# A norm row and a pool-scale row spread by TensorE, gate weights loaded later, two tanh buffers in the tail

## The reference

```python
u = rmsnorm(x, norm_mix);  proj = u @ w_in          # 1024 x 5632
xl, gl, xp, gp, ml, mp = split(proj)
xc = causal_conv(xl)                                # width 4, per channel
r, i = sigmoid(xc @ w_rg_a + b_a), sigmoid(xc @ w_rg_i + b_i)   # 16 blocks of 64x64
log_a = -8 * r * softplus(-lam);  a = exp(log_a)
b = sqrt(1 - a*a) * i * xc;  h = scan(a, b)         # h_t = a_t h_(t-1) + b_t
lru_out = h * silu(gl)
pooled = trailing means of xp over 2/4/8/16 frames, minus xp
pool_out = (pooled @ w_pool + b_pool) * pool_scale * silu(gp)
merged = sigmoid(ml) * lru_out + sigmoid(mp) * pool_out
x = x + merged @ w_out
x = x + sigmoid(rmsnorm(x, norm_ple) @ w_ple_gate) * (p @ w_ple)
y = rmsnorm(x, final_norm)
```

## Time and profile before

| | |
|---|---|
| median of 3 runs shown | 1083.83 us (1073.97 to 1114.7) |
| the profiled execution, its own time | 1074.5 us |
| its span on the slowest core (core 7) | 1072.9 us; the eight cores 1061.6 to 1072.9 |
| busy share of the span | PE 90%, DVE 81%, ACT 74%, POOL 49% |
| mean granted TensorE clock | 0.964 to 0.971 on the eight cores |
| moved by DMA | 188.5 MB per core, 176 GB/s over the span |

### The profile page before, as it was taken

One profiled execution on the slowest core, in us unless ns is written; L12 is line 12 of the kernel. 1 busy time (PEld: TensorE's weight loads), 2 busy tenths in 40 slices (PEclk: granted clock), 3 DMA queues, 4 the chain that ended last, 5 costly groups with the idle time before them and its releaser, 6 DMA issues.

```text
span 1072.9 us, 17836 instructions; the slowest of 8 cores (1061.6 to 1072.9 us)
## 1 busy us (share of the span) xinstructions
PE 963.2 (90%) x4655; PEld 442.4 (41%) x4655; DVE 869.9 (81%) x1224; ACT 796.2 (74%) x1299; POOL 521.4 (49%) x621
## 2 busy tenths in 40 slices
PE   1588988985799999999999999999999999999892
PEld 1233433432344445444444444454444454444340
DVE  3447878897468898899989998899988898979752
ACT  4468888875368888887888778888788877688442
POOL 2113334433336664566554555555666546545554
PEclk9888999988899999999999999999999999999996
DMA  7897798556767784668566475657466655453441
GB/s 220 200 206 227 208 236 231 158 158 199 170 184 210 190 235 124 174 179 215 162 180 175 134 224 158 184 160 198 145 188 166 173 166 160 123 181 119 128 101 78
DMA packets 186663, 188.54 MB, mean 176 GB/s; under 512 B 81273, under 2 KB 131705, under 8 KB 186565
## 3 DMA queue, kind: packets, MB, share of 16 engines
q1 hardware_dynamic: 184981, 184.26, 61.3%
q0 software_dynamic: 1440, 2.62, 1.7%
q10 hardware_dynamic: 144, 0.52, 0.2%
HBM read 143.50 MB, written 29.12 MB: 161 GB/s over the span
## 4 chain that ended last, share of the span: by engine, by line
PE 67%; DVE 8%; issue 6%; ACT 6%; SPq 4%; POOL 4%; DMA 3%; DVEq 0%; ACTq 0%; POOLq 0%
PE psum L675 44%; PE psum L1267 9%; PE psum L1223 9%; SPq L625 3%; PE psum L1287 2%; DVE wk L832 2%; DMA xs<-xp 1%; PE psum L1103 1%; PE psum L876 1%; PE psum L878 1%; POOL xs L1303 1%; DVE wk L1123 1%; POOL mg L1139 1%; ACT wk L915 1%; DVE ub L725 1%
## 5 line engine op out<-in xcount | busy, mean ns | idle before, releaser
L675 PE MATMUL psum<-ut,wr 128*128 128x512 bf16 x2816 | 652.9, 386 | 34.1 <-ACT wk L1110 14.9
L675 PEld LDWEIGHTS psum<-ut,wr 128*128 128x128 bf16 x2816 | 276.7, 99 | 371.0 <-issue 60.5
L832 DVE SCALAR_TENSOR_TENSOR wk<-xlw,cvec,wk 128x512 f32<-128x512 f32 x192 | 203.4, 1059 | 31.9 <-ACT wk L806 8.3
L685 POOL TENSOR_TENSOR stat<-stat,negh 128x1 f32<-128x1 f32 x99 | 73.3, 741 | 257.6 <-DVE stat L682 249.1
L1303 POOL TENSOR_TENSOR xrt<-xrt 128x1024 f32<-128x1024 f32 x30 | 79.2, 2640 | 108.6 <-DVE xrt L1295 108.6
L1267 PE MATMUL psum<-wpg,u2t 128*128 128x512 bf16 x528 | 122.8, 386 | 6.1 <-DMA u2t<-u 6.1
L1223 PE MATMUL psum<-wout,mg 128*128 128x512 bf16 x512 | 117.7, 384 | 11.2 <-POOL mg L1139 11.2
L1139 POOL TENSOR_TENSOR mg<-mg,wk 128x512 bf16<-128x512 bf16 x64 | 95.6, 1494 | 41.6 <-DVE wk L1129 34.8
L959 POOL TENSOR_TENSOR mg<-wk 128x512 bf16<-128x512 f32 x64 | 92.7, 1449 | 0.0
L1245 ACT ACTIVATE junk<-xrt 128x1024 bf16<-128x1024 f32 x60 | 63.6, 1060 | 33.9 <-DVE xrt L1231 17.7
L1267 PEld LDWEIGHTS psum<-wpg,u2t 128*128 128x128 bf16 x528 | 52.1, 99 | 70.2 <-issue 11.5
(11 more groups left out here) (161 smaller groups left out, 1481.8 us busy)
## 6 DMA issues: line engine op xcount, KB each, us to landing
wr<-win_bf SPq DMA_DIRECT2D x264, 256.0 KB, 3.3
xrt<-xp SPq DMA_DIRECT2D x31, 512.0 KB, 5.0
...
```

Of the source, the lines that this page charges most:

```text
L675: P.op("pe", lambda e, kc=kc: e.matmul(bank.ap[:, col:col + N], lhsT=wv[:, kc, :], rhs=ut_v[:, kc, :], start=(kc == 0), stop=(kc == 7)), r ...
L685: P.op("pool", lambda e: e.tensor_tensor(out=st.ap[:, 1:2], in0=st.ap[:, 2:3], in1=NEGH.ap, op=ALU.pow), reads=[st.buf, NEGH.buf], writes= ...
L832: P.op("dve", lambda e, j=j, k=k: e.scalar_tensor_tensor(out=acc_v, in0=xlw_v[:, :, 3 - j:3 - j + L], scalar=CV.ap[:, CW + k * 8 + c:CW + ...
```

## The change

Five edits.

1. `norm_mix` is loaded as one row of 4 KB into partition 0 of `G3` (first DMA on SP), and the new `spread` multiplies a column of 128 ones (in `P32[0]`, set by POOL) with it: two 1x128 by 1x512 fp32 matmuls into two PSUM banks, which DVE copies into `G1BC`. The DMA on ACT's queue goes.
2. `pool_scale` is loaded as one row too; `setup_wpool` spreads it in the same way and multiplies `w_pool` by it straight from PSUM, in two instructions of 512 columns instead of one of 1024.
3. `small_loads` moves from -3.1 to -3.0, behind the two chunk loads at -3.05.
4. In the last four `c_tile`s (`tail`), every other block writes its tanh to `MG0ST[0]`, which lies over half of `MG[0]`, and the second residual add is on DVE instead of POOL.
5. Nearly every number of `OFF` changes, most of them by less than 0.2 of a slot, and the state output of the last tile (`so`) moves from 10.31 to 12.08 slots behind its tile's start.

```diff
-OFF = {0: {'halo': -0.0962, 'copy': 0.0496, 'save': 0.6277, 'gl': 0.2291, 'conv': 0.1245, ...
+OFF = {0: {'halo': -0.5618, 'copy': 0.0597, 'save': 0.5928, 'gl': 0.1655, 'conv': 0.1166, ...
...
+    P.dma(lambda e: e.dma_start(out=G3.ap[0:1, :], in_=d_norm_mix[0:1]), lane=G3.buf, writes=[G3.buf])
     load_x(0)
     load_x(1)
-    P.dma(lambda e: e.dma_start(out=G1BC.ap, in_=d_norm_mix[0].partition_broadcast(128)), lane=G1BC.buf,
-          writes=[G1BC.buf], queue="act")
...
+    P.op("pool", lambda e: e.memset(P32[0].ap[0:1, 0:128], 1.0), writes=[P32[0].buf])
...
+    def spread(row, rowb):
+        bks = [newbank(), newbank()]
+        for hf in range(2):
+            P.op("pe", lambda e, hf=hf: e.matmul(bks[hf].ap, lhsT=P32[0].ap[0:1, 0:128],
+                                                 rhs=row[0:1, hf * 512:(hf + 1) * 512], start=True, stop=True),
+                 reads=[P32[0].buf] + rowb, writes=[bks[hf].buf])
+        return bks
+
+    bks_ = spread(G3.ap, [G3.buf])
+    for hf in range(2):
+        P.op("dve", lambda e, hf=hf: e.tensor_copy(out=G1BC.ap[:, hf * 512:(hf + 1) * 512], in_=bks_[hf].ap),
+             reads=[bks_[hf].buf], writes=[G1BC.buf])
...
-        P.dma(lambda e: e.dma_start(out=pb_ap, in_=d_pool_scale[0].partition_broadcast(128)), lane=pb_b[0],
-              writes=pb_b)
+        P.dma(lambda e: e.dma_start(out=pb_ap[0:1, :], in_=d_pool_scale[0:1]), lane=pb_b[0], writes=pb_b)
...
-        P.op("dve", lambda e: e.tensor_tensor(out=WPOOL.ap, in0=pa_ap, in1=pb_ap, op=ALU.mult),
-             reads=pa_b + pb_b, writes=[WPOOL.buf])
+        bks = spread(pb_ap, pb_b)
+        for hf in range(2):
+            P.op("dve", lambda e, hf=hf: e.tensor_tensor(out=WPOOL.ap[:, hf * 512:(hf + 1) * 512],
+                                                         in0=pa_ap[:, hf * 512:(hf + 1) * 512], in1=bks[hf].ap,
+                                                         op=ALU.mult), reads=pa_b + [bks[hf].buf],
+                 writes=[WPOOL.buf])
...
-        tg = TGC
+        tail = pi >= 29
+        tg = MG0ST[0] if tail and pi % 2 == 1 else TGC
+        tgw = [tg.buf] + (MGB[0][0:4] if tg is not TGC else [])
...
-            P.op("pool", lambda e: e.tensor_tensor(out=xr.ap, in0=xr.ap, in1=tg.ap, op=ALU.add),
+            P.op("dve" if tail else "pool",
+                 lambda e: e.tensor_tensor(out=xr.ap, in0=xr.ap, in1=tg.ap, op=ALU.add),
...
-    state_out(tiles[7], base(tiles[7]) + 10.31)
+    state_out(tiles[7], base(tiles[7]) + OFF[3]["so"])
...
-    at(-3.1, small_loads)
+    at(-3.0, small_loads)
     at(-3.05, lambda: [chunk_load() for _ in range(2)])
```

More of the change, by code:

```diff
@@ L459, in build_program @@
     P.op("dve", lambda e: e.tensor_copy(out=IDB.ap, in_=IDF.ap), reads=[IDF.buf], writes=[IDB.buf])
+    def spread(row, rowb):
[9 more added lines that the diff above has]
+             reads=[bks_[hf].buf], writes=[G1BC.buf])
+    relbank(*bks_)
     vs = WORK[11]
@@ L572, in setup_wpool @@
         done.add("wp")
-        P.op("dve", lambda e: e.tensor_tensor(out=WPOOL.ap, in0=pa_ap, in1=pb_ap, op=ALU.mult),
-             reads=pa_b + pb_b, writes=[WPOOL.buf])
+        bks = spread(pb_ap, pb_b)
[4 more added lines that the diff above has]
+                 writes=[WPOOL.buf])
+        relbank(*bks)
         wk_free["p"].extend([4, 5, 6, 7])
@@ L1277, in f_th @@
                                                           func=AF.Tanh, scale=st.ap[:, 1:2]),
-                     reads=[eb[hf].buf, st.buf], writes=[tg.buf])
+                     reads=[eb[hf].buf, st.buf], writes=tgw)
             relbank(*eb)
```

25 lines of the change are left out of this document (12 added, 13 removed), and 7 rows, old and new, of the table OFF.

## The result

The changed kernel took 1048.67 us (median of 4 runs, 1045.51 to 1051.15), the kernel before 1079.22 (median of 4, 1073.97 to 1114.7). The ratio is 0.973, 95% interval 0.967 to 0.979. Profiled execution against profiled execution it is 1047.63 against 1074.5 us: 27 us less, where I had forecast 18.3. The time lies inside the range given; I had put 0.61 on "within 2%" and 0.37 on what came.

What follows compares the result with a forecast made beforehand. PE's matmuls bound 284 to 1003 us, so gains lie outside. Start-up -4.8, ring 0, passage -6, steady +1 and tail -8.5 sum to -18.3, taking 1074.5 to 1056.2 us; range 1043 to 1073.

Steps and rivals of the forecast that it cites:

- Start-up: Up to 84 us: less DMA time before and in the load-bound stretch, -4.8 us, bounds +2.5 and -8.4.
- the two loads: Start-up: one-row loads of norm_mix and pool_scale free 4.8 us of DMA time, all taken as gain at 84 us.
- the second spread: Start-up, about 70 us: spreading pool_scale in front of running matmuls costs PE +0.5 us at most.
- Edit 3: Start-up: later gate weights move PE's restart from 41.2 to some 43.7 us, while the next stall, at L747, shrinks.
- Ring: 100 to 250 us, PE, DVE and ACT all busy: the new order taken as 0, bounds -4 and +4 us.
- Rival A: More comes through: early PE start holds and one L1110 wait goes between 100 and 250 us; 1048.9 us, chance 0.19.
- Passage: 250 to 284 us: waits for mg 3.7 us and for u2t 2.2 us shorter; taken as -6, bounds -10 and 0.
- Steady: 284 to 1003 us, PE busy nearly throughout: changed order fractions cost +1 us, bounds 0 and +30.
- Rival C: 284 to 1003 us: squares between square roots force ACT table loads, half showing on PE; 1086 us, chance 0.07.
- Tail: From about 1003 us to the end: earlier matmuls and shorter closing links, -8.5 us, bounds -4 and -11.
- The second buffer: Closing blocks: a second tanh buffer gives nothing by itself, since the norm's square on ACT still precedes the next tanh.
- The head: Around 1010 to 1023 us: the later state output removes PE's 3.9 us wait at the state transpose; -2.6 us.

Runs made afterwards that it cites:

- the repeat: The changed kernel run once more, unaltered, on another chip than its first runs: 1045.46 us, ratio to the kernel before 0.976.
- group 3: Changed kernel with OFF's start-up loads and casts, w_ple_gate conversions and base offsets of the first output items as before: ratio to the kernel before 0.979.
- groups 0 and 1: Changed kernel with OFF's entries for the mixer items as before, and one tanh buffer in the tail: 1058.87 us in one run.
- group 2: Changed kernel with OFF's entries for the steps of the output items as before: 1046.59 us in one run.

## Why the prediction was right, and where it was not

**Start-up, -4.8 forecast, -3.9 measured.** The sum is near by luck, its terms are not. "I take the whole 4.8 us as gain" from the two loads held: PE's wait for its chunk ends 5.0 us sooner. The step that failed is the price of the second spread, "+0.5 us at most". It cost 3.8, since a one-row fp32 product takes 1.9 us at the clock it meets, half of the full one behind a stall; the nearest row I had, 0.42 us for a 128x92x128 product, stood for the first spread and was not applied to the second. So loads and spreads together gave 1 us (+1.3 at the mark, +0.9 in core span with the loads back). Edit 3 was right in kind: its stall moved and the sum stayed, 0.6 us. The wait for L747 went for the reason given, ACT's copies ahead of the casts, and was met again at the loaded DMA as I had said, though as DVE's conv steps held behind a cast. The gain that stood in for the loads' is the order's: alone it brought the start-up to 78.7. The start-ups of the first profiles are long for both kernels: before, the mean of its eight spans is 1068.1 us, against 1064.9 to 1066.1 as the usual core span, and the changed kernel's is 1042.3 against 1037.6 in the repeat.

**Ring, 0 forecast, -6.3 measured.** The one large miss, 2 us past its bound of -4. The step that failed is "I take 0": I read the ring by its longest wait (14.9 us for L1110) and called the rest even. What moved were short waits for `xcb`, mostly under 3 us each, whose row stood right below the last one of the earlier trace rows in its view:

```profile
PE psum L876 <- ACT xcb L839: 6.0, 8, 1.6
```

and 5.9 us of DVE's time, 4.3 of them instructions that POOL's products had made longer, up to sixfold. The prediction looked at no instruction's length in the ring. Rival A, at 1048.9 us the case nearest the result, had this stretch gaining 3.7 us, but by the wrong wait.

**Passage, -6 forecast, -2.5 measured, -3.8 in the repeat.** Both places are right, both steps failed. "2.0 + 1.0 + 0.7 = 3.7 us" at the wait for `mg`: it went from 11.2 to 10.3 on core 7, 10.7 to 10.3 as a median. PE reached the wait sooner by what the ring gained, and what POOL's last product waits for came sooner by as much; L604 and L714 were not what set its end: with L604 back at its old place (group 3) the wait is 10.8 us. What sets it was not tried by itself; with the old order of the mixer items (groups 0 and 1) it is 13.2. "The transpose now passes that load: 2.2 us": on core 7

```profile
254.07 0.69 DVE L1259 CAST u<-xrt 128x1024 bf16<-128x1024 f32 x1
...
255.40 1.22 SPq L751 DMA_TRANSPOSE ut<-ub  x1
256.71 1.97 SPq L1276 DMA_TRANSPOSE u2t<-u  x1
```

it is issued 2.6 us after its cast began, where it was 3.0: it passed the load and stands behind the transpose of `ut`, which I had not followed on SP. The wait is 3.1 us on this core and was 6.1; the rest of that came from other steps that got shorter (PE's restart to the cast 4.5 us, was 5.25; the transpose's issue to PE's next product 5.0, was 5.8) and from 1.1 us of other work that PE now does in it.

**Steady, +1 forecast, -2.7 measured.** The +1 stood on no row, and what gave the 2.7 us is open: with group 2 or group 3 back the stretch stays at 717, with groups 0 and 1 back it is 725.7. Rival C is dead: 32 table loads before L920 as before, with a square between two square roots. The table-set rule of the Trainium skill ("ScalarE: Activation LUTs", section on table sets) did not come to bear on the square.

**Tail, -8.5 forecast, -11.6 measured.** The end was right in kind: tanh periods 2.05 us shorter and the end 2.1, -6.8 against -5.9, and the tail of before put back costs 6.9. The second buffer gives nothing by itself, shown with one buffer. The head's size (-2.6) and its reason failed: not the moved state output (0.2 us) but the order of the items, which made the last state and `mg` ready sooner.

**In all.** The forecast of 1056.2 lay 8.6 us over the profiled 1047.6: the ring 6.3, the steady part 3.7, the head 2.2 and the chain 0.9 too high, the passage 3.5 and the start-up 0.9 too low. Ring and steady part were terms of the order table alone, where I had no wait to point at and wrote 0 and +1. That the errors partly cancel (too little in the ring, the steady part and the head, too much in the passage) is luck. Open stays how the ring's gain divides between DVE's longer instructions and the conv steps' place, and what makes the stretch up to the first o-matmul and the head, where no group of the table does it alone.
